# Gate and up projections of a SwiGLU block: from weights as the moving operand to weights standing still

## The reference, cut to what matters

```python
def rmsnorm(x, g):
    y = xf * lax.rsqrt(jnp.mean(xf * xf, axis=-1, keepdims=True) + EPS)
    return y * g

def swiglu(h, w_gate, w_up, w_down):          # (1024, 2816), (1024, 2816), (2816, 1024)
    return (jax.nn.silu(h @ w_gate) * (h @ w_up)) @ w_down

x = x + 0.5 * rmsnorm(swiglu(rmsnorm(x, pre_g), w_gate, w_up, w_down), post_g)
```

## Time and profile before

| what | value |
|---|---|
| median of 3 runs | 1218.79 us (1218.64 to 1218.84) |
| the profiled execution, its own time | 1218.08 us |
| its span, first to last instruction | 1216.0 us |
| TensorE busy | 1199.8 us, 99% |
| VectorE, ScalarE, GpSimd busy | 800.2, 671.7, 160.8 us |
| mean granted TensorE clock | 0.999 of full speed |
| HBM | 217.93 MB read, 180 GB/s over the span |

### The profile page before, as it was taken

One profiled execution on the slowest core, in us unless ns is written; L12 is line 12 of the kernel. 1 busy time (PEld: TensorE's weight loads), 2 busy tenths in 40 slices (PEclk: granted clock), 3 DMA queues, 4 the chain that ended last, 5 costly groups with the idle time before them and its releaser, 6 DMA issues.

```text
span 1216.0 us, 19442 instructions
## 1 busy us (share of the span) xinstructions
PE 1199.8 (99%) x6120; PEld 1009.0 (83%) x6120; DVE 800.2 (66%) x1214; ACT 671.7 (55%) x1117; POOL 160.8 (13%) x282
## 2 busy tenths in 40 slices
PE   7999999999999999999999999999999999999997
PEld 5888888779898888888888888887899988888886
DVE  6776646797656676665476665478866566666655
ACT  6555545656555565553475554377556355555544
POOL 1000001673110100000010000036532001000001
PEclk9999999999999999999999999999999999999999
DMA  8555565453554365555465555554535444555563
GB/s 340 194 186 194 178 209 173 167 190 120 175 174 146 132 205 177 184 205 194 161 210 177 196 197 191 190 202 153 180 119 180 157 147 154 179 195 173 200 209 128
DMA packets 32916, 220.06 MB, mean 181 GB/s; under 512 B 4272, under 2 KB 4528, under 8 KB 8768
## 3 DMA queue, kind: packets, MB, share of 16 engines
q1 hardware_dynamic: 32544, 218.98, 52.9%
q10 hardware_dynamic: 288, 0.02, 0.0%
HBM read 217.93 MB, written 1.05 MB: 180 GB/s over the span
## 4 chain that ended last, share of the span: by engine, by line
PE 95%; DVE 2%; issue 1%; POOL 1%; DMA 0%; ACT 0%; DVEq 0%; ACTq 0%; POOLq 0%
PE acc L470 29%; PE acc L472 29%; PE acc L471 29%; PE tb L531 4%; PE mb L623 1%; PE mb L765 1%; PE acc L781 1%; DVE w_lo L1187 1%; DMA inv_f<-in_inv_freq 0%; PE mb L716 0%; PE mb L700 0%; DVE xT_lo L1193 0%; PE mb L685 0%; PE mb L660 0%; PE mb L471 0%
## 5 line engine op out<-in xcount | busy, mean ns | idle before, releaser
L1187 DVE SCALAR_TENSOR_TENSOR w_lo<-raw,gains,w_hi 128x512 fp32r<-128x512 f32 x580 | 417.3, 781 | 44.7 <-ACT w_hi L874 44.1
L470 PE MATMUL acc<-w_hi,xT_hi 128*128 128x512 f32 x1024 | 406.5, 397 | 3.7 <-DVE w_lo L1575 3.5
L874 ACT ACTIVATE w_hi<-raw,gains 128x512 fp32r<-128x512 f32 x580 | 370.2, 713 | 65.0 <-PE acc L472 64.8
L471 PE MATMUL acc<-w_lo,xT_hi 128*128 128x512 f32 x1024 | 399.9, 390 | 0.0
L472 PE MATMUL acc<-w_hi,xT_lo 128*128 128x512 f32 x1024 | 399.8, 390 | 0.0
L470 PEld LDWEIGHTS acc<-w_hi,xT_hi 128*128 128x128 f32 x1024 | 192.8, 188 | 46.2 <-DVE w_lo L1575 3.9
L472 PEld LDWEIGHTS acc<-w_hi,xT_lo 128*128 128x128 f32 x1024 | 192.8, 188 | 40.8
L471 PEld LDWEIGHTS acc<-w_lo,xT_hi 128*128 128x128 f32 x1024 | 193.0, 188 | 37.8
L1181 DVE TENSOR_TENSOR w_lo<-raw,w_hi 128x1024 fp32r<-128x1024 f32 x112 | 123.9, 1146 | 71.9 <-ACT w_hi L868 70.8
L868 ACT ACTIVATE w_hi<-raw 128x1024 fp32r<-128x1024 f32 x112 | 105.6, 990 | 76.0 <-PE acc L472 76.0
L939 ACT ACTIVATE th<-acc,stats 128x256 f32<-128x256 f32 x88 | 41.8, 475 | 189.1 <-PE acc L472 188.0
(11 more groups left out here) (172 smaller groups left out, 1236.7 us busy)
## 6 DMA issues: line engine op xcount, KB each, us to landing
raw<-in_gu SPq DMA_DIRECT2D x92, 1024.0 KB, 5.1
raw<-in_down SPq DMA_DIRECT2D x32, 1024.0 KB, 5.0
raw<-in_in SPq DMA_DIRECT2D x24, 1024.0 KB, 5.2
raw<-in_kv SPq DMA_DIRECT2D x16, 1024.0 KB, 5.1
raw<-in_down SPq DMA_DIRECT2D x16, 768.0 KB, 4.2
raw<-in_out SPq DMA_DIRECT2D x8, 1024.0 KB, 5.1
raw<-in_q SPq DMA_DIRECT2D x8, 1024.0 KB, 5.2
raw<-in_o SPq DMA_DIRECT2D x8, 1024.0 KB, 5.2
```

The lines of the kernel that those rows point to most:

```text
L470: pe.matmul(o, st_hi, mv_hi, start=first, stop=False)
L471: pe.matmul(o, st_hi, mv_lo, start=False, stop=False)
L874: act.activation(w_hi[:, slot, k, :], raw[:, slot, k, :], ACT.Copy, scale=gains[:, ds(g, 1)]).then_inc(s_hi, 1)
L1187: dve.scalar_tensor_tensor(w_lo[:, slot, k, :], raw[:, slot, k, :], gains[:, ds(g, 1)], w_hi[:, slot, k, :].bitcast(F32), ALU.mult, ALU.su ...
```

## The change

Chunks 0 and 1 stay as they are. In chunks 2 to 10 the operands change places: 128 weight columns are the stationary operand and the transposed input moves. A chunk has four passes, in this order: gate features 0 to 127, the up features that belong to them, gate features 128 to 255, their up features. In a pass, for each k, `w_hi` stands still while the high and the low input move past it in one matmul of 512 columns (`xT` now holds them side by side), and `w_lo` stands still while the high input alone moves, 256 columns, added to the second half of the bank. So a bank ends with hi·hi in its first 256 columns and the two low products in its second 256, features in the partitions, tokens along the row. A pair of passes (gate and up of 128 features) uses two of the four banks.

What follows a pair: ScalarE copies the low halves of both banks to `gu` (`low_products`), VectorE adds the first halves to them and frees the banks (`sums`), GpSimd multiplies by the row of token factors `r_all` and makes the product of up and gate (`products`: three instructions), ScalarE takes tanh (`feature_tanh`), VectorE makes (tanh + 1)·product (`hidden`), ScalarE writes it to `hT_hi` (`feature_hi`), VectorE writes `hT_lo` (`hidden_lo`). No transposes of chunks 2 to 10. The row `r_all` is made once per FFN by two matmuls behind the transposes of chunks 0 and 1, all of them between the first and the second pass of chunk 2 (`behind_tokens`). The splits are dealt out anew: of the second half of a chunk the first two k are split one body earlier than the last two. A slot's first half is now free in the fourth pass of its chunk, at seven eighths of it, where it was free at three quarters.

```diff
-        xT_hi = sb("xT_hi", [P, KD, TOK], F32R)
-        xT_lo = sb("xT_lo", [P, KD, TOK], F32R)
+        xT = sb("xT", [P, KD, 2, TOK], F32R)
+        xT_hi, xT_lo = xT[:, :, 0, :], xT[:, :, 1, :]
...
@@ TensorE
+                def behind_tokens():
+                    for j in range(TOK_CH):
+                        h_transposes(l, f, j)
+                    n = t_no(l, ("r", f))
+                    pe.wait_ge(s_tev, n - 1)
+                    pe.wait_ge(s_rpre, l * 8 + 2 * phase + 1 + 1)
+                    for t in range(TT):
+                        mm = pe.matmul(tb[t_bank(("r", f))][:, t * P:(t + 1) * P],
+                                       r_pre[:, t:t + 1].to_broadcast([P, P]), ident[:, :], start=True, stop=True)
+                    mm.then_inc(s_t, 1)
+                def feature_chunk(j, i=0, behind=None):
+                    ci = c0 + j
+                    for b in range(4):
+                        if b == 1 and behind is not None:
+                            behind()
+                        q, t = feat_q(f, j, b), b % 2
+                        wait_acc(l, q, t, 2 * i)
+                        o = acc[q % 2][t]
+                        c = b % 2 * 256 + b // 2 * P
+                        for k in range(KD):
+                            h, kk = k // 4, k % 4
+                            slot = (2 * ci + h) % 4
+                            if b == 0:
+                                pe.wait_ge(s_lo, 4 * half_no(l, ci, h) + 4 * i * 4 + kk + 1)
+                            pe.matmul(o[:, :], w_hi[:, slot, kk, c:c + P], xT[:, k, :, :].rearrange("p a i -> p (a i)"),
+                                      start=k == 0, stop=False)
+                            mm = pe.matmul(o[:, TOK:2 * TOK], w_lo[:, slot, kk, c:c + P], xT_hi[:, k, :],
+                                           start=False, stop=k == KD - 1)
+                            if b == 3 and k == 3:
+                                mm.then_inc(s_half, 1)
+                        mm.then_inc(s_acc, 1)
...
@@ ScalarE
+                def body(j, i=None):
+                    low_products(j, 0, i)
+                    split_hi(l, c0 + j + 1, 1, i, ks=(2, 3), parts=(1,))
+                    feature_tanh(j, 0, i)
+                    feature_hi(j, 0, i)
+                    low_products(j, 1, i)
                     split_hi(l, c0 + j + 2, 0, i)
+                    feature_tanh(j, 1, i)
+                    if j + 1 < FU:
+                        split_hi(l, c0 + j + 2, 1, i, ks=(0, 1), parts=(0,))
+                    feature_hi(j, 1, i)
...
@@ VectorE
+                def sums(j, p, i):
+                    n = pair_no(l, f, j, p, i) + 1
+                    q = feat_q(f, j, 2 * p)
+                    dve.wait_ge(s_low, n)
+                    for b in range(2):
+                        dve.tensor_tensor(gu[:, p, b, :], acc[q % 2][b][:, 0:TOK], gu[:, p, b, :],
+                                          ALU.add).then_inc(s_accf[bank(q, b)], 1)
+                def hidden(j, p, i):
+                    n = pair_no(l, f, j, p, i) + 1
+                    dve.wait_ge(s_fth, n)
+                    dve.wait_ge(s_prod, n)
+                    dve.scalar_tensor_tensor(gt[:, p, :], th[:, p, :], 1.0, gu[:, p, 1, :], ALU.add,
+                                             ALU.mult).then_inc(s_fh, 1)
...
+                def body(j, i=None):
+                    sums(j, 0, i)
+                    split_lo(l, c0 + j + 1, 1, i, ks=(2, 3), parts=(1,))
+                    hidden(j, 0, i)
+                    hidden_lo(j, 0, i)
+                    sums(j, 1, i)
                     split_lo(l, c0 + j + 2, 0, i)
+                    hidden(j, 1, i)
+                    if j + 1 < FU:
+                        split_lo(l, c0 + j + 2, 1, i, ks=(0, 1), parts=(0,))
+                    hidden_lo(j, 1, i)
...
@@ GpSimd, for each pair p of chunk j
+                        for b in range(2):
+                            pool.wait_ge(s_accf[bank(q, b)], acc_uses(l, q) + 1 + 2 * x)
+                        pool.tensor_tensor(gu[:, p, 0, :], gu[:, p, 0, :], r_all[:, 0, :], ALU.mult).then_inc(s_arg, 1)
+                        pool.tensor_tensor(gu[:, p, 1, :], gu[:, p, 1, :], r_all[:, 1, :], ALU.mult).then_inc(s_up, 1)
+                        pool.wait_ge(s_up, n)
+                        pool.tensor_tensor(gu[:, p, 1, :], gu[:, p, 1, :], gu[:, p, 0, :],
+                                           ALU.mult).then_inc(s_prod, 1)
```

More of the change, by code:

```diff
@@ L120 @@
 T_USES += [("x", 3, t, a) for t, a in XUSE]
-T_USES += [("h", 1, j) for j in range(FU)]
+T_USES += [("h", 1, j) for j in range(TOK_CH)] + [("r", 1)]
 T_USES += [("x", 4, 0, 0), ("x", 4, 0, 1)]
@@ L578, in ffn @@
+                feature_chunk(TOK_CH, behind=behind_tokens)
                 with pe.Fori(0, (FU - 5) // 2) as i:
                     for p in range(2):
-                        up(2 + p, i)
-                for j in range(FU - 3, FU):
-                    up(j)
+                        feature_chunk(3 + p, i)
+                for j in range(FU - 2, FU):
+                    feature_chunk(j)
                 for d, (n, k0, nk) in enumerate(DOWN[:4]):
@@ L871, in split_hi @@
                 act.nop(nofuse=True)
-                for k in range(nk):
+                for k in range(nk) if ks is None else ks:
                     g = lay * (N_GAINS * KD) + gain * KD + h * nk + k
@@ L952, in ffn @@
+                tanh(0, 0)
+                tanh(1, 0)
                 split_hi(l, c0 + 2, 0)
-                tanh(0, 1, None)
+                tanh(0, 1)
                 split_hi(l, c0 + 2, 1)
-                tanh(1, 1, None)
+                tanh(1, 1)
                 split_hi(l, c0 + 3, 0)
+                h_hi(0)
+                h_hi(1)
+                split_hi(l, c0 + 3, 1, ks=(0, 1))
+                body(2)
                 with act.Fori(0, (FU - 5) // 2) as i:
                     for p in range(2):
-                        up(2 + p, i)
@@ L960, in ffn @@
[L960 to L961 removed]
+                        body(3 + p, i)
+                for j in range(FU - 2, FU):
+                    body(j)
                 for d in range(6):
                     ci = c0 + FU + d
[L964 to L965 removed]
                     if d == 3:
[L967 to L968 removed]
+                        y_square(l, phase, q0 + Q_DOWN, 0, 0)
+                        y_square(l, phase, q0 + Q_DOWN, 0, 1)
@@ L1279, in ffn @@
+                dve.tensor_copy(r_all[:, 1, :], src).then_inc(s_tev, 1)
+                split_lo(l, c0 + 3, 1, ks=(0, 1))
+                body(2)
                 with dve.Fori(0, (FU - 5) // 2) as i:
                     for p in range(2):
-                        up(2 + p, i)
-                for j in range(FU - 3, FU):
-                    up(j)
+                        body(3 + p, i)
+                for j in range(FU - 2, FU):
+                    body(j)
                 for d in range(6):
@@ L1631, in pre, with products, body @@
                 pool.tensor_tensor(c_half[:, c], r_half[:, c], r_pre[:, c], ALU.mult).then_inc(s_rpre, 1)
+            def products(l, f):
+                pool.wait_ge(s_tev, t_no(l, ("r", f)) + 1)
+                def body(j, i=None):
+                    for p in range(2):
+                        n = pair_no(l, f, j, p, i) + 1
+                        q = feat_q(f, j, 2 * p)
+                        x = 0 if i is None else i
+                        for b in range(2):
+                            pool.wait_ge(s_accf[bank(q, b)], acc_uses(l, q) + 1 + 2 * x)
[4 more added lines that the diff above has]
+                                           ALU.mult).then_inc(s_prod, 1)
+                body(2)
+                with pool.Fori(0, (FU - 5) // 2) as i:
+                    for p in range(2):
+                        body(3 + p, i)
+                for j in range(FU - 2, FU):
+                    body(j)
             def rope(l, t):
@@ L1740, in _ @@
                 pre(l, 0, 1)
+                products(l, 0)
                 post(l, 0, 0)
@@ L1752, in _ @@
                 pre(l, 3, 1)
+                products(l, 1)
                 post(l, 3, 0)
```

162 lines of the change are left out of this document (87 added, 75 removed).

## The result

The changed kernel takes 1243.43 us (median of 4 runs, 1242.79 to 1243.93) against 1218.72: ratio 1.0204, 95% interval 1.019 to 1.0219. The profiled execution took 1243.93 us, its span is 1242.1. The forecast was 1226 us: the direction was right and the time inside the range, but 7 us more were forecast where 25 more came.

A forecast was written before the change was run, and what follows sets the result against it. TensorE, busy 99% of the span, was taken to bound the kernel. 1218.08 - 8.1 + 1.2 + 5.4 + 4 x 2.2 = 1225.4 us for the profiled execution, 0.7 under the median, so 1226.1 us; range 1213 to 1248.

The forecast's parts named there:

- What bounds the kernel, and the count of matmuls: TensorE, busy 99% of the span, bounds; a chunk goes from 48 matmuls to 64 with as many columns.
- The spacing: On TensorE, one k costs 0.2267 + 0.1200 = 0.347 us, a chunk 11.09 against 11.32.
- the 8.1 us that the change was to save on TensorE: Over 36 chunks, transposes removed save 15.8 us, 16 more matmuls a chunk cost 7.7; net -8.1 us.
- The row of token factors: In chunk 2, its matmuls cost 1.2 us in all; TensorE stands still 1.35 us before them, 5.4 in four FFNs.
- That the queues' lap decides, with VectorE and GpSimd blocking each other: Chunks 2 to 10: the queues' time per chunk is 12.0 us against TensorE's 11.1, with 0.42 lost per GpSimd product.
- The stall in each FFN: TensorE waits ahead of first passes in the last chunks: 2.0 us, plus 0.2 for the first down pass.
- the 4 x 2.2 us of the sum: The term for TensorE's stalls behind the queues' lap, 2.2 us in each of four FFNs.
- a time of 1243, for longer handing over: Alternative in the queues: 0.06 us more at each of about ten steps is 0.6 a lap, 1243 us.
- The queues keep pace: Rival: lap at most 11.68 us, so TensorE is not delayed by it; 1217.3 us, chance 0.20.
- Blocking for the whole instruction: Rival: each GpSimd product costs VectorE 0.73 us, lap 13.2, 1261 us; chance 0.15, shared with other waits in the body.
- Cheaper matmuls: Rival: the short matmul's 13.3 ns hide behind the long one, saving 15.4 us; 1202 or 1224 us, chance 0.10.

The follow-up runs named there:

- e1: Changed kernel with the VectorE splits of chunks 2 to 10 reading a PSUM bank instead of w_hi as second operand; 1222.56 us, ratio 1.0024.
- e2: Changed kernel without GpSimd's multiplication of up by the token factor, two products a pair instead of three; 1220.92 us, ratio 1.0019.
- e3: Changed kernel with a pair's hidden, feature_hi and hidden_lo moved behind the next pair's sums on ScalarE and VectorE; 1221.32 us, ratio 1.0024.
- e6: e3 with chunk 0's transposes and the token-factor row between passes one and two of chunk 2, chunk 1's between two and three; 1218.52 us, 1.0002.

## Why the prediction missed, step by step

**What bounds the kernel, and the count of matmuls: right.** As many columns, 64 matmuls a chunk, no transposes. **The spacing: too low.** I added two spacings, 0.347 us a k, and put the unknown only below it. In the profiled stages of e1, e2, e3 and e6, where TensorE never waits for `sums`, it is 0.3533 in thirteen and 0.3467 in three. At 0.3533 a chunk is 11.31 us against 11.32 before: of the 8.1 us that the change was to save on TensorE next to nothing is left, even if nothing ever waits. In the changed kernel this is not seen in the time, because the lap is longer; in e1, e2, e3 and e6 it is.

**The row of token factors: mechanism and place right.** The gap is 1.27 and 1.19 us for the 1.35 forecast, ended by VectorE's low copy. The row's matmuls cost 0.46 us instead of 0.22: the profile counts four for the two in the code.

**That the queues' lap decides, with VectorE and GpSimd blocking each other: right, and shown by e1.** The FFN's splits went above 747 ns, the product beside a split to 1.1 and 1.2. The size was off. Blocking is 0.49 for each product ((4.11 - 2.63)/3), not 0.42: 0.2 us a lap. The trace of the kernel before had this figure: my 0.42 is the mean over one multiplication and two subtractions of GpSimd, and the split that met the multiplication, at 248.64, took 1.23 us, 0.49 above its 0.74, the others 1.10 and 1.15. The FFN's products are all multiplications. (Why a subtraction costs less was not tested.) Handing over is 0.04 to 0.16 rather than 0.03, so the first pair's part is 0.2 longer. Lap 12.41 instead of 11.97.

**The stall in each FFN: the step that failed.** The term is the 4 x 2.2 us of the sum. By it the first down pass starts 104.6 us after chunk 2; it starts after 109.1. Two things are wrong in it. The larger is the size of the lap, which counts seven times. The other is a path that I did not see. I let chunk 10 wait for the seventh lap and then let the down chunks begin when chunk 10 was done, with 0.2 us for `hidden_lo`. But the first down pass uses the same bank again and needs the sums of chunk 10's first pair, an eighth lap: 12.41 after the seventh, where I had allowed 11.3 (chunk 10 and the 0.2). Per FFN the miss is 7 x 0.44 = 3.1 (the lap) + 1.1 (the eighth) + 0.3 (first sums 9.85 instead of 9.55, most of it the row's matmuls) = 4.5 us; 4 x 4.5 = 18 us. On the 1225.4 of the profiled execution that makes 1243.4, where its own time was 1243.9. I had written that each 0.1 of lap costs 2.8 us and added up the lap from bare durations; by that rule a lap of 12.41 gives 1238, and the eighth lap is what is missing.

**What was luck.** The forecast also has a time of 1243, for longer handing over. It wanted a lap of 12.6 for it; at the real lap of 12.41 the same time needs the eighth lap. And the measured time lies in the stated range because the range was wide, not because the sum was near.

**The rivals.** *The queues keep pace* did not happen, but e3 makes it happen by order alone: it gives 1221.3, where the forecast said 1217.3; some 3.5 us of that is the spacing of 0.3533 in two stages of its profiled execution. *Blocking for the whole instruction* (lap 13.2, 1261) is refuted at that price: 0.49 us are lost for a product of 0.74. What came is milder: the instructions of the two end in turns, 0.55 to 0.60 us apart, as if they excluded each other for that part of their 0.74 us. With its second input in PSUM the split took 740 ns beside the products, and the products 0.74 us: no blocking at all (e1). That agrees with the Trainium skill, "SBUF — State Buffer", section "Who interferes with whom", by which a VectorE instruction with at most one SBUF input, outside the modes that use two ports, does not contend with GpSimd. *Cheaper matmuls* did not come: the lowest spacing seen in turns, 0.3467, is the sum.

## What to carry to other kernels

Work moved to other engines is not hidden because each has idle time: add up one lap of the queues, waits included, and compare it with the bound engine's period. If it is longer, the time at which the buffer first comes free plus one lap for every reuse, also the one by the stage that follows, is when the stage can end; set it against what the bound engine needs alone. Where a lap is a row of waits between engines, put the dependent half behind the next item's independent work before giving any up; here that was worth 22 us of 25. If two engines read SBUF side by side, take their durations from a place in the trace where they do, with the same kind of instruction on both.

## What the runs showed of the hardware that was not expected

The same instructions run at one of two spacings for a whole stage. In e3, one execution, stages 1 and 3 (102.7 us) have 15 k between these two starts of long matmuls, 5.20 us, 0.3467 a k; stages 2 and 4 (104.5 us) 17 in 6.01, 0.3535 (0.3533 over the stage):

```profile
68.72 0.39 PE L626 MATMUL acc<-xT,w_hi 128*128 128x512 f32 x1
...
73.92 0.39 PE L626 MATMUL acc<-xT,w_hi 128*128 128x512 f32 x1
```

```profile
469.77 0.40 PE L626 MATMUL acc<-xT,w_hi 128*128 128x512 f32 x1
...
475.78 0.40 PE L626 MATMUL acc<-xT,w_hi 128*128 128x512 f32 x1
```

The first FFN of both layers is one piece of code, and in e2 it ran at 0.3533 in the first layer and 0.3467 in the second, so it is not the code. In the changed kernel, where TensorE is stopped before each late chunk, the spacing changes between these two values from chunk to chunk. Most changes come at a restart, but not all: at 126.9 us, inside chunk 9, it goes from 0.3467 to 0.3533 with no start more than 15 ns late. What sets it was not found. It makes some 2 us a stage. That would be enough for the spread of e1 (1220.3 to 1224.7), whose profiled execution, the slowest, has 0.3533 in all four stages; the faster ones have no trace, so this is not shown.
